# The last down product of a two-layer network on one TensorE core, run, added and stored by halves of 256 tokens

## The reference

```python
def sqrelu_mlp(x, w_up, w_down):
    return jnp.square(jax.nn.relu(x @ w_up)) @ w_down

def second_block(x, ...):
    h = x
    for l in range(DEPTH):                       # DEPTH = 2
        ...                                      # l = 0: recurrent block, l = 1: attention, both added to h
        h = h + sqrelu_mlp(rmsnorm_2(h, mlp_norm[l]), w_up[l], w_down[l])
    return h
```

## Time and profile before

| | |
|---|---|
| runs | 2770.67, 2770.86, 2772.41 us; median 2770.86 us |
| profiled execution | span 2767.5 us from the first to the last instruction; the page gives no other time of it |
| median of the runs less that span | 3.4 us |
| busy share of the span | PE 99%, PEld 80%, DVE 44%, ACT 38%, POOL 46% |
| mean granted TensorE clock | 0.999 of full speed |
| matmuls and weight loads in the trace | 12570 of each |
| DMA | 259 MB, mean 94 GB/s |

### The profile page before, as it was taken

One profiled execution on the slowest core, in us unless ns is written; L12 is line 12 of the kernel. 1 busy time (PEld: TensorE's weight loads), 2 busy tenths in 40 slices (PEclk: granted clock), 3 DMA queues, 4 the chain that ended last, 5 costly groups with the idle time before them and its releaser, 6 DMA issues. The chain is left out here.

```text
span 2767.5 us, 34707 instructions
## 1 busy us (share of the span) xinstructions
PE 2737.1 (99%) x12570; PEld 2224.9 (80%) x12570; DVE 1221.9 (44%) x1607; ACT 1064.6 (38%) x1567; POOL 1273.4 (46%) x984
## 2 busy tenths in 40 slices
PE   9999999999999999999999999999999998999999
PEld 7777887888877788787888877888888876788887
DVE  6755555212247645555221268643324237443222
ACT  4444434322343444434222248433224338533222
POOL 5455453444454554553444445454444432354443
PEclk9999999999999999999999999999999999999999
DMA  4333332333333333332333333333333220233333
GB/s 144 95 102 100 92 93 76 99 99 94 97 100 92 99 99 98 98 93 75 95 99 99 93 91 93 98 92 99 99 93 128 83 77 16 65 96 95 95 99 99
DMA packets 72699, 259.17 MB, mean 94 GB/s; under 512 B 8192, under 2 KB 9088, under 8 KB 72448
## 3 DMA queue, kind: packets, MB, share of 16 engines
q1 hardware_dynamic: 71280, 254.17, 30.9%
q10 hardware_dynamic: 1296, 3.28, 0.3%
HBM read 255.31 MB, written 2.10 MB: 93 GB/s over the span
## 5 line engine op out<-in xcount | busy, mean ns | idle before, releaser
L363 POOL TENSOR_TENSOR w_lo<-w_raw,w_hi 128x512 fp32r<-128x512 f32 x476 | 628.3, 1320 | 1406.8 <-ACT w_hi L389 1405.8
L855 PE MATMUL ps<-H_hi,w_hi 128*128 128x512 f32 x2240 | 899.5, 402 | 8.0 <-DVE H_lo L1395 3.7
L857 PE MATMUL ps<-H_hi,w_lo 128*128 128x512 f32 x2240 | 873.5, 390 | 0.0
L856 PE MATMUL ps<-H_lo,w_hi 128*128 128x512 f32 x2240 | 873.1, 390 | 0.0
L389 ACT ACTIVATE w_hi<-w_raw 128x1024 fp32r<-128x1024 f32 x476 | 499.8, 1055 | 565.9 <-DMA w_raw<-w_all 565.8
L365 POOL TENSOR_TENSOR w_lo<-w_raw,w_hi 128x512 fp32r<-128x512 f32 x476 | 651.5, 1369 | 0.0
L855 PEld LDWEIGHTS ps<-H_hi,w_hi 128*128 128x128 f32 x2240 | 420.8, 188 | 114.0 <-issue 21.4
L856 PEld LDWEIGHTS ps<-H_lo,w_hi 128*128 128x128 f32 x2240 | 420.9, 188 | 97.1 <-issue 13.2
L857 PEld LDWEIGHTS ps<-H_hi,w_lo 128*128 128x128 f32 x2240 | 420.6, 188 | 88.4
L855 PE MATMUL ps<-Y_hi,w_hi 128*128 128x512 f32 x1168 | 457.6, 392 | 5.9 <-DVE Y_lo L1887 2.1
L857 PE MATMUL ps<-Y_hi,w_lo 128*128 128x512 f32 x1168 | 455.1, 390 | 0.0
(11 more groups left out here) (271 smaller groups left out, 2483.9 us busy)
## 6 DMA issues: line engine op xcount, KB each, us to landing
w_raw<-w_all SPq DMA_DIRECT2D x476, 512.0 KB, 3.6
X<-xT SPq DMA_DIRECT2D x8, 256.0 KB, 5.6
rel_bias<-bias ACTq DMA_DIRECT2D x1, 2048.0 KB, 8.8
outT<-X SPq DMA_DIRECT2D x8, 256.0 KB, 3.1
sguw<-sgu_wT ACTq DMA_DIRECT2D x2, 256.0 KB, 3.2
CS<-cossin SPq DMA_DIRECT2D x1, 256.0 KB, 7.8
sgub<-sgu_b ACTq DMA_DIRECT2D x2, 128.0 KB, 3.1
sgug<-sgu_g ACTq DMA_DIRECT2D x2, 128.0 KB, 3.2
```

What stands on the lines that cost most here:

```text
L363: nc.gpsimd.tensor_tensor(w_lo[:, s, 0:UNIT // 2], w_raw[:, s, 0:UNIT // 2], f(w_hi[:, s, 0:UNIT // 2]), ALU.subtract).then_inc(w_lo_half, 1)
L855: MM(out, wh, xh, start=start, stop=False)
L856: MM(out, wh, xl, start=False, stop=False)
L857: return MM(out, wl, xh, start=False, stop=stop)
```

## The change

The eight down units of the last quarter of the last network are cut by tokens. Each unit runs its eight input tiles for tokens 0 to 255 into bank u % 4, then again for tokens 256 to 511 into bank 4 + u % 4. A unit of 24 matmuls with 512 columns becomes one of 48 matmuls with 256 columns. The end of the first half is told by a new semaphore `half_mm`, the end of the second by `w_used` as before. DVE adds each half to `X` on its own and counts `half_done`, and SP stores each half on its own: 16 stores of 128 KB in place of eight of 256 KB. The last quarter is written out on PE, and the loop there has one iteration less. All earlier quarters, and the network of the other layer, are as they were.

```diff
--- before.py
+++ after.py
@@ -215,6 +215,7 @@
             sem("hn_sq"), sem("hn_mm"), sem("hn_mean"), sem("hn_root"), sem("hn_inv"), sem("hn_row"), sem("hn_turned"), sem("hn_done"))
         inv_ready, scaled_done = sem("inv_ready"), sem("scaled_done")
         bias_loaded = sem("bias_loaded")
+        half_mm, half_done = sem("half_mm"), sem("half_done")
         stored = sem("stored")
 
         def v(name, k=0, n=1):
@@ -331,9 +332,11 @@
                     eng.wait_ge(w_used, i * WSLOTS + (s - WSLOTS + 1))
                     eng.dma_start(w_raw[:, s, :], w_all[bass.ds(i * WSLOTS + s, 1)].rearrange("o p n -> (o p) n")).then_inc(w_loaded[s], 16)
             for k in range(DT):
-                eng.wait_ge(x_done, XDONE["mlp1"] + k + 1)
-                eng.dma_start(outT[k * P:(k + 1) * P, :], X[:, k, :]).then_inc(stored, 16)
-            eng.wait_ge(stored, 16 * DT)
+                for half in range(2):
+                    t = slice(half * 256, half * 256 + 256)
+                    eng.wait_ge(half_done, 2 * k + half + 1)
+                    eng.dma_start(outT[k * P:(k + 1) * P, t], X[:, k, t]).then_inc(stored, 16)
+            eng.wait_ge(stored, 32 * DT)
 
 
         @block.gpsimd
@@ -1241,8 +1244,24 @@
             together(UAO, 3, Yh, Yl, SPLIT["lru"], None, late=1)
             gemm(UAO + 3, DT - 3, Yh, Yl)
 
+            def unit_by_halves(u, xh, xl, tiles, free, ready=None):
+
+                pe.wait_ge(w_lo_ready, u + 1)
+                pe.wait_ge(unit_out, free)
+                s = u % WSLOTS
+                for half in range(2):
+                    t = slice(half * 256, half * 256 + 256)
+                    for k in range(tiles):
+                        if ready is not None and half == 0:
+                            pe.wait_ge(lo_ready, ready + k + 1)
+                        m = three(ps[:, 4 * half + u % 4, t], w_hi[:, s, k * P:(k + 1) * P], w_lo[:, s, k * P:(k + 1) * P],
+                                  xh(k)[:, t], xl(k)[:, t], k == 0, k == tiles - 1)
+                    if half == 0:
+                        m.then_inc(half_mm, 1)
+                m.then_inc(w_used, 1)
+
             def mlp(n, U0):
-                def quarter(i, first):
+                def quarter(i, first, halves=False):
                     for j in range(8):
                         unit(i * 16 + (U0 + j), U0 + j, ps[:, (U0 + j) % 4, :], Hh, Hl, 8, i * 16 + (U0 + j - 3),
                              SPLIT[f"mlp_in{n}"] if first and j == 0 else None)
@@ -1250,10 +1269,15 @@
                             norm(f"mlp{n}")
                     for m in range(8):
                         c = U0 + 8 + m
+                        if halves:
+                            unit_by_halves(i * 16 + c, Yh, Yl, 8, i * 16 + (c - 3), None if m else i * 8 + SPLIT[f"mlp{n}"])
+                            continue
                         unit(i * 16 + c, c, ps[:, c % 4, :], Yh, Yl, 8, i * 16 + (c - 3), None if m else i * 8 + SPLIT[f"mlp{n}"])
                 quarter(0, True)
-                with pe.Fori(1, QUARTERS) as i:
+                with pe.Fori(1, QUARTERS if n == 0 else QUARTERS - 1) as i:
                     quarter(i, False)
+                if n:
+                    quarter(QUARTERS - 1, False, True)
             mlp(0, UM0)
             def head_sums(i):
 
@@ -1872,6 +1896,18 @@
                 add_squares("mlp0", k)
                 x_lo("mlp_in0", "mlp0", k)
 
+            def add_half_to_x(u, m):
+
+                for half in range(2):
+                    t = slice(half * 256, half * 256 + 256)
+                    if half == 0:
+                        dve.wait_ge(half_mm, m + 1)
+                    else:
+                        dve.wait_ge(w_used, u + 1)
+                    VE.tensor_tensor(X[:, m, t], X[:, m, t], ps[:, 4 * half + u % 4, t], ALU.add).then_inc(half_done, 1)
+                    dve.wait_ge(half_done, 2 * m + half + 1)
+                dve.sem_inc(unit_out, 1)
+
             def mlp(n, U0):
                 link(root(f"mlp{n}", RS[:]))
 
@@ -1897,7 +1933,11 @@
                 looped(QUARTERS - 1, 8, body)
                 ups(QUARTERS - 1, link)
                 for m in range(8):
-                    add_to_x(U0 + 16 * (QUARTERS - 1) + 8 + m, m, f"mlp{n}")
+                    u = U0 + 16 * (QUARTERS - 1) + 8 + m
+                    if n:
+                        add_half_to_x(u, m)
+                        continue
+                    add_to_x(u, m, f"mlp{n}")
                     if n == 0:
                         add_squares("kv_norm", m)
                         x_lo("kv_norm", "kv_norm", m)

```

## The result

The changed kernel takes 2775.18 us (median of 20 runs, 2773.63 to 2776.14) against 2770.64 us of the kernel before (20 runs, 2769.75 to 2772.43): 4.54 us more. The ratio is 1.0015, with a 95% interval of 1.0008 to 1.0021, which is 2.2 to 5.8 us. The forecast was +4.0 us. The loss is real. The measured 0.16% lies inside the 0.2% (5.5 us) that the prediction counted as no change; the upper end of the interval is just over it.

What follows compares the result with a forecast made beforehand. TensorE's matmul rate was taken to bound the kernel. Matmuls (2.6) and a wait (1.9) add 4.47 us, the tail saves 0.47: +4.0 us, from 2770.86 to 2774.9 us, range 2770.5 to 2779.0.

Steps and rivals of the forecast that it cites:

- The rate: Last quarter's down matmuls: 256 columns start 0.120 us apart, 0.0133 above streaming per matmul; with the wait, chance 0.50.
- the first rival: Down matmuls: the extra goes with columns, 0.1133 us each, +1.6 us in all, 2772.4; chance 0.20.
- the row of 0.110: Profile row of eight plain float32 matmuls of 128 columns, starting 0.110 us apart, taken as nearest to 256-column fp32r.
- The load as the bound: Down matmuls: weight load (0.112) outlasts streaming (0.107), so about 0.126 us each, +6.2 us, 2777.0; chance 0.22.
- The load that is not hidden: Down matmuls: weight load not overlapped, 0.216 to 0.219 us each, about 2810 us; chance 0.05.
- The wait: First down unit: TensorE reaches `Y_lo` tile 7 early, at 2723.19, and stands some 1.8 us; 1.9 of the loss.
- the restart: First down unit, behind the tile 7 pause: a load with nothing to hide behind adds 0.11 us.
- The clock: TensorE behind the tile 7 pause: stays at 1.00, as through an earlier pause of over 1 us.
- The block: Last quarter's down matmuls to the end of streaming: +4.47 us, 2.6 from matmuls and 1.9 from waiting.
- The tail: Last add and store: 0.27 us saved on the add, 0.2 on the landing, -0.47 us, between -0.27 and -0.62.
- The sum: Whole kernel: +4.47 less 0.47, so +4.0 us; span 2771.5, median 2774.9.
- the second case: Extra goes with columns, not matmuls; at its low 0.109 us a matmul, 0.0 in all, 2770.9; chance 0.20.

Runs made afterwards that it cites:

- quarters: Changed kernel with the last quarter's eight down units cut to 768 matmuls of 128 columns, adds and stores by halves: 2890.23 us in a single run, against 2771.4.
- the run by tiles: Changed kernel, but its first down unit takes both halves of an input tile before the next tile: 2772.62 us against 2771.4 (ratio 1.0006).
- Two experiments that remove it: Changed kernel with the first down unit whole (512 columns): 2772.29 us against 2771.12; or with that unit's halves ordered tile by tile: 2772.62 against 2771.4.
- quarters without the wait: Changed kernel with the first down unit whole and the other seven in four passes of 128 columns: 2806.84 us in a single run, against 2770.71.
- the matmuls alone by halves: Changed kernel with both 256-column halves in one PSUM bank, each unit added and stored whole: 2775.64 us against 2771.12 (ratio 1.0017).
- The adds and stores alone: Changed kernel with matmuls whole as before, only adds and stores by halves behind each unit's last matmul: 2770.53 us against 2771.12 (ratio 0.9999).

## Why the prediction was right

- *The rate.* Forecast 0.120 us for 256 columns, measured 0.1200. With 0.2267 for 512, the difference of 256 columns is 0.1067, pure streaming at 2.4 GHz, and 0.0133 is left for each matmul at both widths: a price of each matmul, not of each column. That settles the first rival (0.1133); the row of 0.110 that spoke for it is one of transposes (L960), not of products. The load as the bound (0.126) falls too, by 0.1200 here and by 0.1116 in quarters. The load that is not hidden (0.219) is off by far. The 192 added matmuls cost 192 x 0.0133 = 2.6 us, as forecast; the run by tiles shows them with the tail's gain taken off, +2.05.
- *Beside the skill.* 0.112 us of load and 0.107 of streaming are done every 0.120 us. The Trainium skill's formula for a warm matmul alone ("TensorE: Matmul & The Clock Gate", "Back-to-back issue gap") gives, as an estimate, 109 ns for 256 columns, 11 ns under what this form takes. The Trainium skill's rule in Part 3 of the same page, that loads overlap with matmuls in flight only in another row group, does not hold here; in the same part the Trainium skill also lets a load for the background weight buffer go ahead, which the prediction left out.
- *The wait.* Forecast 1.8 us for tile 7, and 0.11 for the restart. Measured 2727.76 - 2725.95 = 1.81, and the next start 0.23 later where it is 0.12 elsewhere, 0.11 more. Two experiments that remove it get 2.16 (with one unit less in halves, worth 0.3) and 1.88 back.
- *The clock, partly by luck.* It stayed at 1.00 behind the wait, as forecast. The forecast took that from one pause, of just over 1 us, and gave a fall neither a price nor a chance. The same trace has another, of 1.45 us and ahead of short matmuls, behind which the clock was at half for some 7 us (the line below, in the columns of the earlier trace rows); all ten traces show a fall there. And a pause of 1.9 us between matmuls of 512 columns, near 139 us, is in all ten traces: in seven the clock stayed, in three it fell (the rows are in the last section). So that the clock stays behind one pause doesn't show that it will behind another. A fall cost 1.6 us there; as an estimate that much more here would have made +5.6 us.

```profile
2295.40:2302.30 6.90, 5.98 (x28) 4.00 (x28) 3.94 (x8) 6.89 (x21) 0.00 (x0) 0.51 0.01 2
```
- *The block.* To the end of the streaming, 47.86 + 0.12 = 47.98 against 43.29 + 0.23 = 43.52: +4.46, where the forecast said +4.47.
- *The tail.* The add took 0.42, as forecast. The store landed in 1.7 and not 2.0; I had taken 0.2 of the 0.3. Behind the streaming, 2774.2 - 2771.42 = 2.78 against 3.31: -0.53, where the forecast said -0.47.
- *The sum.* +3.93 in the trace, +4.0 forecast. The median of the runs moved by 4.54, with an interval that holds both. That last 0.5 us can't be read: the median of before itself lay between 2770.64 and 2771.40 in four rounds.
- *A step that did not matter.* I read 3.4 us between span and median as what lies around the span. The profiled execution of the changed kernel took 2775.96 us for its span of 2774.2, so 1.8 lie around it; the rest was that the profiled execution of before was a quick one (the runs of before on record have spans from 2767.5 to 2770.9). The forecast put the difference on the median and so was not touched by it; the span that it named, 2771.5, was missed by 2.7.
- *The lower edge of the range.* 2770.5 is called the low end of the second case, whose sum is 2770.9, or 2770.7 with the largest tail. Nothing hung on it.

## What to carry to other kernels

Cutting the end of an accumulation, so that taking the sum out of PSUM and storing it overlap with the rest, gains only where there is a tail, that is in the last unit, and most if only its last matmuls are cut: by the traces six matmuls more gained 0.48 us and 24 more 0.18, where 192 more lost 3.9. A narrower matmul keeps the price that each has beyond its columns (0.0133 us here), and it didn't go under the load of its weights (0.112). And whoever makes a consumer reach its inputs sooner must look up when the last of them is made: the 0.5 us of slack at tile 7 was in the trace, and turned into 1.9 us of waiting.

## What the runs showed that I had not expected

The run in quarters stood for 1.9 us, went on with 128 columns, and lost half its clock from 1.2 us later to the end: some 75 us on top of the price of the narrow form (the 156.8 us from 2728.6 to the last start, 0.213 a matmul, would be 82 at 0.1116). The weight loads slow down with the clock: the starts are 0.213 apart, though 128 columns at 1.2 GHz need only 0.107. The changed kernel stood for 1.7 us, went on with 256 columns, and kept its clock; quarters without the wait kept it too.

That looks as if pause and narrow matmuls together had brought the clock down, but the traces don't show it. The same fall comes with matmuls of 512 columns behind a pause of the same length, and not in every execution. These are the rows of the pause near 139 us, in the trace of before, then in that of the matmuls alone by halves, where nothing has been changed yet:

```profile
139.38 0.47 PE L855 MATMUL ps<-H_hi,w_hi 128*128 128x512 f32 x1 [1.89 <-POOL w_lo L365]
...
140.84 0.40 PE L855 MATMUL ps<-H_hi,w_hi 128*128 128x512 f32 x1
141.07 0.39 PE L856 MATMUL ps<-H_lo,w_hi 128*128 128x512 f32 x1
```

```profile
139.39 0.47 PE L856 MATMUL ps<-H_hi,w_hi 128*128 128x512 f32 x1 [1.89 <-POOL w_lo L366]
...
140.83 0.63 PE L858 MATMUL ps<-H_hi,w_lo 128*128 128x512 f32 x1
141.26 0.63 PE L856 MATMUL ps<-H_hi,w_hi 128*128 128x512 f32 x1
...
143.80 0.39 PE L856 MATMUL ps<-H_hi,w_hi 128*128 128x512 f32 x1
144.03 0.40 PE L857 MATMUL ps<-H_lo,w_hi 128*128 128x512 f32 x1
```

The starts go from 0.23 apart to 0.43 about 1 us behind the pause, and back at 143.80. The adds and stores alone and the quarters with the first unit whole show the same there; the other seven traces keep 1.00. What is peculiar to the run in quarters is thus not the fall but that the clock stayed down for 157 us of gapless work, where every other fall in the ten traces before the last matmul was over within 7 us. Whether the 128 columns kept it down is open: it is one run, and it was not repeated.

The 2.8 us by which F differs between before and after come in two steps, both long before the change. The stretch of 14 to 22 us in the trace of before, then in that of after:

```profile
14.00:22.00 8.00, 7.11 (x30) 5.12 (x29) 6.95 (x8) 4.39 (x8) 5.23 (x4) 1.00 0.36 113
```

```profile
14.00:22.00 8.00, 6.46 (x20) 4.51 (x19) 6.95 (x8) 3.83 (x7) 4.51 (x4) 0.79 0.27 91
```

With the same instructions, the clock is 1.00 in one execution and 0.79 in the other, and 30 matmuls are done against 20. Late inputs came first: TensorE waited for `H_lo` twice, 0.82 and 0.72 us, and the matmul that starts at 15.88 before starts at 17.10 after, 1.2 us late, while the clock falls only at about 17.8. From 28 us on the two are 2.05 apart. Another 0.9 come at 395 us, where before doesn't have to wait and after does:

```profile
395.46 0.50 PE L855 MATMUL ps<-M_hi,w_hi 128*128 128x512 f32 x1
```

```profile
398.42 0.50 PE L858 MATMUL ps<-M_hi,w_hi 128*128 128x512 f32 x1 [0.77 <-DVE M_lo L1604]
```

Why those inputs were late was not tried. F lies between 2720.67 and 2724.15 in the ten traces, though the same instructions run ahead of it. This is why effects under 2 us were read from F on, and not from spans.
